# Expert rows added by TensorE with diagonal gates, all tiles gathered early, and a channel norm in two groups

## What is computed

```python
def conv_module(xn, ...):
    a, g = split(xn @ w_pw1 + b_pw1)
    u = a * sigmoid(g)
    dw = causal depthwise conv of width 31 over (state, u)
    z = silu(layer_norm(dw, ln_g, ln_b))     # over the 1024 channels
    return z @ w_pw2 + b_pw2

def hier_moe(xn, ...):   # 4 groups of 8 experts, 2 experts a row
    y[n] = sum over the row's two experts e of
           gate[n, e] * ((silu(xn @ w_gate[e]) * (xn @ w_up[e])) @ w_down[e])

x = x + mixer(rms_norm(x));  x = x + hier_moe(rms_norm(x))     # both layers
y = rms_norm(x)
```

## Time and profile before

| | us |
|---|---|
| median of three runs | 1279.34 |
| lowest and highest | 1275.59, 1279.53 |
| the profiled execution, its own time | 1276.34 |
| its span, first to last instruction | 1274.7 |
| TensorE busy in the span | 1076.6 |
| VectorE busy | 493.8 |
| ScalarE busy | 289.6 |
| Pool busy | 271.8 |

### The profile page before, as it was taken

One profiled execution on the slowest core, in us unless ns is written; L12 is line 12 of the kernel. 1 busy time (PEld: TensorE's weight loads), 2 busy tenths in 40 slices (PEclk: granted clock), 3 DMA queues, 4 the chain that ended last, 5 costly groups with the idle time before them and its releaser, 6 DMA issues.

```text
span 1274.7 us, 14566 instructions
## 1 busy us (share of the span) xinstructions
PE 1076.6 (84%) x5326; PEld 626.3 (49%) x5326; DVE 493.8 (39%) x1066; ACT 289.6 (23%) x616; POOL 271.8 (21%) x289
## 2 busy tenths in 40 slices
PE   6999999999996879888765999987987978787780
PEld 5777777774545333333325777743545333233320
DVE  3244444444356111111116699994555111111116
ACT  3233232233111101000003455554111101000002
POOL 3000000001002211111032388860003111011033
PEclk9999999999997999888886999998996989888995
DMA  8953322302706999999955922100027999999973
GB/s 273 387 182 110 109 93 77 103 30 106 298 34 225 398 419 420 420 421 421 418 188 137 363 66 66 34 24 1 34 84 280 411 420 420 421 419 421 397 269 131
DMA packets 107791, 303.67 MB, mean 238 GB/s; under 512 B 18248, under 2 KB 65480, under 8 KB 82745
## 3 DMA queue, kind: packets, MB, share of 16 engines
q1 hardware_dynamic: 85481, 254.74, 51.7%
q0 software_dynamic: 22256, 48.22, 10.5%
HBM read 278.34 MB, written 57.12 MB: 263 GB/s over the span
## 4 chain that ended last, share of the span: by engine, by line
PE 58%; DMA 21%; DVE 10%; issue 8%; ACT 2%; SPq 1%; POOL 0%; DVEq 0%; POOLq 0%
DMA ring<-in_w_up 16%; PE bank L1205 12%; PE bank L522 10%; PE bank L421 7%; PE bank L1222 7%; PE bank L549 4%; DVE bank L1688 2%; PE bank L1484 2%; PE bank L572 2%; PE bank L1195 2%; PE bank L588 2%; PE bank L613 2%; PE bank L346 1%; DMA work<-in_w_pw 1%; PE bank L954 1%
## 5 line engine op out<-in xcount | busy, mean ns | idle before, releaser
L1205 PE MATMUL bank<-ring,work 128*64 128x512 f32 x704 | 171.2, 642 | 30.9 <-DMA ring<-in_w_up 29.1
L1222 PE MATMUL bank<-ring,work 128*64 128x512 f32 x528 | 127.9, 629 | 37.1 <-DVE work L1241 21.6
L1484 PE MATMUL bank<-arena,work 128*128 128x288 f32 x512 | 129.4, 415 | 8.4 <-issue 4.0
L522 PE MATMUL bank<-arena,ring 128*128 128x288 f32 x512 | 131.9, 412 | 0.0
L1205 PEld LDWEIGHTS bank<-ring,work 128*64 128x64 f32 x704 | 60.6, 147 | 138.9 <-issue 136.6
L1237 DVE TENSOR_TENSOR work<-work,bank 128x256 f32<-128x256 f32 x33 | 13.9, 421 | 287.3 <-ACT work L1233 287.3
L1484 PEld LDWEIGHTS bank<-arena,work 128*128 128x128 f32 x512 | 99.1, 195 | 38.2 <-issue 8.4
L1635 POOL TENSOR_TENSOR ring<-ring 128x606 f32<-128x606 f32 x76 | 103.8, 1365 | 55.6 <-ACT ring L1584 46.0
L522 PEld LDWEIGHTS bank<-arena,ring 128*128 128x128 f32 x512 | 94.9, 190 | 32.6 <-issue 7.9
L421 PE MATMUL bank<-ring,arena 128*128 128x512 f32 x224 | 101.1, 605 | 6.6 <-ACT arena L1619 6.6
L1205 PE MATMUL bank<-arena,work 128*64 128x512 f32 x352 | 86.5, 648 | 17.1 <-DMA arena<-in_w_up 16.1
(11 more groups left out here) (258 smaller groups left out, 1299.6 us busy)
## 6 DMA issues: line engine op xcount, KB each, us to landing
ring<-in_w_down SPq DMA_DIRECT2D x32, 2048.0 KB, 24.2
ring<-in_w_gate SPq DMA_DIRECT2D x22, 2048.0 KB, 21.6
ring<-in_w_up SPq DMA_DIRECT2D x22, 2048.0 KB, 28.2
arena<-in_w_gate SPq DMA_DIRECT2D x10, 2048.0 KB, 23.9
arena<-in_w_up SPq DMA_DIRECT2D x10, 2048.0 KB, 31.6
ring<-in_w_qkv SPq DMA_DIRECT2D x24, 512.0 KB, 6.0
y_sorted<-gain POOLq DMA_DIRECT2D x8, 1536.0 KB, 5.7
work<-in_w_pw SPq DMA_DIRECT2D x16, 512.0 KB, 5.1
```

What stands on the lines that cost most here:

```text
L522: mm = nc.tensor.matmul(bank[b][:, 0:HT], wa[s][:, w, c, :], xt[:, c, h * HT:(h + 1) * HT], start=c == 0, stop=c == C - 1)
L1205: mm = nc.tensor.matmul(bank[2 + s][rr, :], xte[s][:, c, rr], wgu[g][:, :, e, c, :], start=c == 0, stop=c == C - 1)
L1222: mm = nc.tensor.matmul(bank[5 + h][rr, :], hts[:, c, rr], wdn[s][:, e, c, h * HALF:(h + 1) * HALF], start=c == 0, stop=c == FC - 1)
L1484: mm = nc.tensor.matmul(bank[banks[h][w]][:, 0:GT], wp[s][:, w, c, :], xt[:, c, h * GT:(h + 1) * GT], start=c == 0, stop=c == C - 1)
```

## The change

- **Adding the rows.** VectorE builds ten diagonal matrices from the gates (`spread_gates`) when the experts are done. TensorE multiplies them with the gathered rows into PSUM (`mix_pe`: four products of 128x512 a tile), and VectorE adds the sum to x in one pass. TensorE's order in the boundary: sum 0, sum 1, turn 0, sum 2, turn 1, sum 3, turn 2, sum 4, then the gated products; tiles 3 and 4 are turned inside their second half, the small vectors inside the first. VectorE's order: add 0, add 1, norm 0, add 2, norm 1 and so on. ScalarE now copies both halves of the turned tiles.
- **Gathers.** Tile 0's blocks lie in the free end of `arena`, so all ten blocks have a place and are fetched early (tile 4's behind the last store), and ten late gathers follow.
- **Convolution weights.** The buffers in `work` are regrouped so that the first chunk's weights fit once pair 14's first products are done; the second chunk's wait for the last add.
- **Channel norm.** The variance, root, reciprocal, scaling and Silu run over rows 0 to 255, then over rows 256 to 575.
- The warm-up products now start with `extra_end` in both layers, and the table for the root is loaded ahead.

```diff
+        y_at = [[arena[:, FIRST_Y + k * D:FIRST_Y + (k + 1) * D]] +
+                [ring[:, 1, (2 * j + k) * D:(2 * j + k + 1) * D] for j in range(TILES - 1)] for k in range(2)]
...
-        xe = part[0:2]
+        xe = part[0:4:2]
...
+        xte = [a.rearrange("p (c r) -> p c r", c=C) for a in part[1:4:2]]
+        gate_diag = work[:, 2 * D:2 * D + 2 * TILES * P].rearrange("p (k j n) -> p k j n", k=2, j=TILES)
...
         def norms_act(act, steps, n):
+            if n == 2:
+                nc.scalar.activation(warm[:], eps[:], ACT.Sqrt)
+                for j, turn in ((0, None), (1, 0), (2, 1), (3, 2), (4, 3), (None, 4)):
+                    if j is not None:
+                        norm_act(act, steps, n, j)
+                    if turn is not None:
+                        turn_act(act, n, turn)
+                        turn_copy(act, nc.scalar.copy, n, turn, 1, turn_ev_d)
+                return
...
         def norms_dve(dve, steps, n):
+            if n > 0:
+                for j in range(TILES + 1):
+                    if j < TILES:
+                        combine_dve(dve, n // 2 - 1, j)
+                    if j >= 1:
+                        norm_dve(dve, steps, n, j - 1)
+                return
...
-            do(V.tensor_copy(slot[:], slot_f[:]))
...
                 if local == EARLY_PAIRS:
                     pool.wait_ge(further_known, 2 * (l + 1))
+                    pool.wait_ge(far_scattered, 16 * (2 * TILES - FAR_FIRST) * (l + 1))
...
+                    for j in range(TILES - 1):
                         for k in range(2):
+                            y_rows_in(pool, j, k, early_slot)
+            for k in range(2):
+                y_rows_in(pool, TILES - 1, k, early_slot)
...
+                pool.wait_ge(gathered[j], 64 * l + 32)
                 for k in range(2):
+                    y_rows_in(pool, j, k, late_slot)
...
+        def mix_pe(pe, l, j):
             r = rows[j]
+            if j == 0:
+                pe.wait_ge(gates_spread, l + 1)
+            pe.wait_ge(gathered[j], 64 * (l + 1))
+            if j >= 2:
+                pe.wait_ge(combined, TILES * l + j - 1)
+            for h in range(2):
+                for k in range(2):
+                    mm = nc.tensor.matmul(mix_out(j)[:, h * HALF:(h + 1) * HALF], gate_diag[0:r, k, j, 0:r],
+                                          y_at[k][j][0:r, h * HALF:(h + 1) * HALF], start=k == 0, stop=k == 1)
+            mm.then_inc(mixed, 1)
...
+        def combine_dve(dve, l, j):
+            here = x[0:rows[j], j, :]
+            dve.wait_ge(mixed, TILES * l + j + 1)
+            nc.vector.tensor_tensor(here, here, mix_out(j), ALU.add).then_inc(combined, 1)
...
         def experts_pe(pe, l):
...
             extra_turns(pe, l, further)
+            pe.wait_ge(extra_end, l + 1)
+            keep_running(7, 16)
+            if l == LAYERS - 1:
+                for j in range(TILES):
+                    mix_pe(pe, l, j)
...
+            if l == 0:
+                sp.wait_ge(base.gu_mm, EPAIRS - 1)
+                conv_load(sp, 0, 0)
             sp.wait_ge(base.dn_mm, EPAIRS * (l + 1) - 1)
...
         def conv_first(sp):
-            sp.wait_ge(gathered[0], landed(0, 1))
-            conv_load(sp, 0, 0)
+            sp.wait_ge(gathered[0], 64)
...
+            sp.wait_ge(combined, TILES)
             conv_load(sp, 1, 1)
...
-            pe.wait_ge(combined, 1)
-            for j in range(HALF_TILES):
-                keep_running(4 if j else 10)
...
-                turn_pe(pe, 2, j)
+            mix_pe(pe, 0, 0)
+            for j in range(TILES - 1):
+                mix_pe(pe, 0, j + 1)
+                if j < HALF_TILES:
+                    turn_pe(pe, 2, j)
...
             for c in range(C):
                 pe.wait_ge(sq_done, c + 1)
+                mm = variance(c, 0)
+                if c < C - 3:
+                    variance(c, 1)
+            mm.then_inc(var_mm, 1)
+            for c in range(C - 3, C):
+                mm = variance(c, 1)
             mm.then_inc(var_mm, 1)
...
+            for g, (at, end) in enumerate(LN_PARTS):
+                act.wait_ge(var_mm, g + 1)
+                nc.scalar.activation(sig[:, at:end], bank[6 + g][:, 0:end - at], ACT.Sqrt, bias=ln_eps[:]).then_inc(std_done, 1)
+            for g, (at, end) in enumerate(LN_PARTS):
+                for c in range(C):
+                    act.wait_ge(scaled, C * g + c + 1)
+                    nc.scalar.activation(dw[:, c, at:end], dw[:, c, at:end], ACT.Silu, bias=chan[:, c, TAPS + 2:TAPS + 3],
+                                         scale=chan[:, c, TAPS + 1:TAPS + 2]).then_inc(swished, 1)
...
+            for g, (at, end) in enumerate(LN_PARTS):
+                dve.wait_ge(std_done, g + 1)
+                steps.done(V.reciprocal(sig[:, at:end], sig[:, at:end]))
+                for c in range(C):
+                    V.tensor_tensor(dw[:, c, at:end], dw[:, c, at:end], sig[:, at:end], ALU.mult).then_inc(scaled, 1)
```

More of the change, by code:

```diff
@@ L152, in encoder @@
         up_i = sb("up_i", [P, CAP], I32)
-        slot = sb("slot", [P, 2, TILES], I32)
         r_iota = sb("r_iota", [P, CAP])
@@ L1146, in experts_pool @@
                     pool.wait_ge(further_known, 2 * (l + 1))
+                    pool.wait_ge(far_scattered, 16 * (2 * TILES - FAR_FIRST) * (l + 1))
                     pool.wait_ge(base.y_out[0], 16 * (EPAIRS // 2) * (l + 1))
                     pool.wait_ge(base.y_out[1], 16 * (EPAIRS // 2) * (l + 1))
-                    for j in range(TILES):
+                    for j in range(TILES - 1):
                         for k in range(2):
-                            if early(j, k):
-                                y_rows_in(pool, j, k, early_slot)
-        def early(j, k):
-            return k == 0 or j < EARLY_TILES
-        def landed(j, layers, late=True):
-            each = [1 + (late and early(j, k)) if late else early(j, k) for k in range(2)]
-            before = [1 + early(j, k) for k in range(2)]
-            return 16 * (sum(before) * (layers - 1) + sum(each))
+                            y_rows_in(pool, j, k, early_slot)
+            for k in range(2):
+                y_rows_in(pool, TILES - 1, k, early_slot)
         def y_rows_in(pool, j, k, part):
@@ L1171, in gather_pool @@
             for j in range(TILES):
-                pool.wait_ge(gathered[j], landed(j, l + 1, late=False))
+                pool.wait_ge(gathered[j], 64 * l + 32)
                 for k in range(2):
-                    y_rows_in(pool, j, k, late_slot if early(j, k) else slot)
-        def combine_dve(dve, steps, l, j):
-            r = rows[j]
-            dve.wait_ge(gathered[j], landed(j, l + 1))
-            steps.done(nc.vector.scalar_tensor_tensor(x[0:r, j, :], y_at[0][j][0:r, :], gate_w[0:r, 0, j:j + 1],
-                                                      x[0:r, j, :], ALU.mult, ALU.add))
-            nc.vector.scalar_tensor_tensor(x[0:r, j, :], y_at[1][j][0:r, :], gate_w[0:r, 1, j:j + 1],
-                                           x[0:r, j, :], ALU.mult, ALU.add).then_inc(combined, 1)
@@ L1227, in ex_turn_copy @@
             eng.wait_ge(m.xt_mm, i + 1)
-            copy(xte[s][:, 4 * half:4 * half + 4, :], bank[half][:].rearrange("p (c r) -> p c r", c=4)).then_inc(done, 1)
+            copy(xte[s if m is base else 1][:, 4 * half:4 * half + 4, :], bank[half][:].rearrange("p (c r) -> p c r", c=4)).then_inc(done, 1)
         def ex_silu_act(act, m, i, s):
```

86 lines of the change are left out of this document (47 added, 39 removed).

## The result

| | before | after |
|---|---|---|
| median of the runs, us | 1279.43 (1275.59 to 1280.24, 4 runs) | 1291.39 (1290.88 to 1292.33, 4 runs) |
| the profiled execution, us | 1276.34 | 1291.39 |
| its span, us | 1274.7 | 1289.7 |
| TensorE, VectorE busy, us | 1076.6, 493.8 | 1114.2, 482.1 |

The ratio after to before is 1.0091 with a 95% interval of 1.0071 to 1.0111: slower by 12 us between the medians. The profiled execution of before lies 3 us under its median and that of after on its own, so the two traces differ by 15.0 us.

A forecast was written before the change was run, and what follows sets the result against it. Bound taken: waits in the boundary between layers, no engine or transfer full, with VectorE's convolution behind. +14.9 - 6.2 + 2.5 = +11.2 us on the profiled 1276.34 gives 1287.5; 1289 taken for the median, range 1278 to 1300.

The forecast's parts named there:

- boundary and convolution: Between the layers and the convolution behind: later fifth norm delays the second chunk's weights, so the stage loses 14.9 us.
- channel norm: Two groups start the projection 5.15 us earlier and regain half of 2.0 us of clock: gain 6.2 us.
- end: Last layer's five sums on TensorE: last norm 2.5 us late, bounds 1.5 and 5.
- The order of the sums: Boundary: nothing overlaps between TensorE and VectorE; a cycle takes 7.6 us against 4.5, TensorE idle some 3.0 us in each.
- The clock: Boundary: each return of TensorE from three idle gaps costs 2.2 us, 6.6 in all; first gated half does not pay again.
- Rival (a): Clock holds through the three gaps: boundary 8.3, norm 7.2, sum +3.6, about 1281 us; chance 0.12.
- (b): Weights do not bind, the queue's 10 MB go faster: boundary costs 9.9, sum +6.2, 1283 to 1285 us; chance 0.12.
- (d): Clock holds and weights do not bind together: -1.4 us, 1275 to 1278, or an unseen gain; chance 0.10.
- (c): Clock stays at 1.2 GHz through every sum after the gaps: 9 to 12 us more, 1298 to 1301; chance 0.10.
- Two more gathers and the early weights at nothing: Ahead of the late gathers: both cost nothing; other bound, load beside the gathers, 3 us on the last stored rows.
- the late gathers themselves later than before: Sign at the boundary's start that the forecast was wrong: then the early weights cost; no size given.
- The weights bind: Second chunk: 10 MB stream follows the fifth norm, 14.9 us late, and VectorE's wait grows by the difference.

The follow-up runs named there:

- Experiment 2: Changed kernel with each turn one sum later on TensorE (sum 2 ahead of turn 0 and so on): ratio 0.9994 to the kernel before, span 1276.9 us.
- Experiment 3: Changed kernel with nine unit-matrix products in each of TensorE's three waits for a tile's norm: ratio 1.0087 to the kernel before, span 1285.7 us.
- experiment 6: Changed kernel with the last layer's sums back on VectorE, without diagonals and warm-up there: ratio 1.0095 to the kernel before, span 1290.3 us.
- Experiment 10: Changed kernel with the first chunk's convolution weights issued once tile 0's rows are in: ratio 1.0059 to the kernel before, span 1282.5 us.
- experiment 4: Changed kernel with the convolution's small vectors sent after the last tile's gathers: ratio 1.0077 to the kernel before, span 1290.1 us.
- experiment 5: Changed kernel with tile 4's two early gathers issued just ahead of its late ones: ratio 1.0137 to the kernel before, span 1295.3 us.
- experiment 8: Changed kernel with sums back on VectorE in both layers and second chunk's weights not held back: ratio 0.9943 to the kernel before, span 1270.1 us.
- experiment 11: Changed kernel with sums on VectorE, second chunk's weights not held back, small vectors after the last tile's rows: ratio 0.9906 to the kernel before, median 1267.07 us.
- Experiment 1: Kernel before with only the channel norm in two groups: ratio 0.9957 to the kernel before, span 1271.7 us.
- experiment 12: As experiment 11, with the first chunk's weights issued once tile 0's rows are in: ratio 0.9896 to the kernel before, median 1266.65 us.

## Why the prediction was right, and where it was off

The forecast was slower, 1289 us in a range of 1278 to 1300; it is 1291.39. The parts stand against the traces so:

| step | foretold | measured |
|---|---|---|
| boundary and convolution | +14.9 | +20.0 |
| channel norm | -6.2 | -6.7 |
| end | +2.5 | +1.7 |
| sum | +11.2 | +15.0 |

**The order of the sums: right.** The cycle was to be 7.6 us with 3.0 us of idle TensorE; it is 7.3 with 2.71, released by VectorE's norm. The product against a diagonal was put at 0.865 us, 3.46 a tile. It is 3.60 for one tile alone and 3.5 within a block. The add out of PSUM, in no row before, takes 1.22, the lower bound. Experiment 2 takes the cycle away and gets 12 us back, so the mechanism is shown.

**The clock: right in kind, wrong in place and size.** The step was 2.2 us for each of three gaps, 6.6 in all. In the profiled execution the clock held through all three and fell once, behind them: 3.4 us in sum 4 before the first gated product, and 1.7 in that product, which the forecast had said would not pay again. Experiment 3 takes both away. The price of the same gaps was 1.7 to 5.1 us in five executions, so no price per gap fits, and why the clock falls at one of them and not at another stays open. Rival (a), that the clock holds, was right for three cycles and wrong for the last sum. Of (b) and (d) the weights speak: TensorE waited 6.81 us for them. (c) had the clock low through every sum after the gaps. No execution shows this; that of experiment 6 comes nearest, with sums 2 and 3 partly low.

**"Two more gathers and the early weights at nothing": wrong, and the largest error.** The forecast argued from a mean: DMA 0.17 busy at 644 to 648, so the load lies in a hole. It gave 3 us as the other bound and did not take it. The issue of its two transfers took the sync engine 7.4 us from 639.60 on (1.3 before), the late gathers came 1.9 us late, and the forecast's own sign ("the late gathers themselves later than before") was there to see. What it had not seen is the second step. The small vectors wait for tile 0's rows. In the kernel before the weights stand ahead of them on the queue, and they follow tile 1's first gather by 3.1 us. With the weights gone from there they follow it by 1.7, and sum 1 waits 2.48 us and runs slower by 1.8. The first turn ends at 688.95 where 682.5 was foretold: 6.4 us, 2.2 ahead of sum 0 and 4.2 in sum 1. Experiment 10 gives back 7.2 us of span, and experiment 4 gives back sum 1's share alone; experiment 5 says that the two gathers have hardly a part in it (6.85 us behind the store and not 7.1). The rule of the Trainium skill that the forecast cited (DMA: Bandwidth & Descriptors, Queues, rings and completion order: each DMA engine takes turns between the queues that have work) would, by the forecast's bound, have added 3 us, with which the sum would have been 1290.5. The runs here agree with it (the late gathers start 2.4 us later by the early load, 7.1 against 4.7 us behind the store), in sign and nearly in size, though no run shows that it is by taking turns. The choice against it was wrong, and the 3 us would still have left out sum 1's 4.2.

**How the two met.** At the first gated product 6.4 us too little for the start, 3.2 too much for the clock and 0.6 too much for two cycles leave 2.6: it was foretold for 707.8 and began at 710.44. So the 14.4 us there (11.8 foretold) are partly right by cancelling errors. The same holds for the clock: with the 1.8 in sum 1 it cost 6.9 us in all, close to the 6.6 booked, but in other places and in part for another wait.

**The weights bind: right, with 2.0 us missing.** The time from the fifth norm to the second chunk's product was taken as unchanged at 37.0 us. It is 39.0. Of this 1.2 is the second chunk's 1 MB, sent at 711.79 ahead of the router's tables: experiment 8 takes it away. The other 0.8 stays open. The first tap was foretold 9.9 us late (both halves of chunk 0 done at 726.3) and came 14.9 late; as VectorE then waits for the second chunk's weights anyway, this did not change the stage, and its wait grew by 5.2 us where 5.0 follow from the forecast. The fifth norm's terms add up to 712.1, where 712.2 is written. The sum of the boundary is 14.9 + 2.6 + 2.0, and 0.5 more arises up to the variances.

**The channel norm: right.** The projection starts 4.8 us earlier (5.15 foretold) and runs 2.0 us faster (1.0 foretold): all that the clock had cost there came back, not half. It does not in every execution: behind the same 2.6 us of idle time the projection took 22.3 to 22.4 us in experiments 4, 6 and 11, and 20.84 in the ten other traces. ScalarE's Silu begins at 888.18, where the table load of 1.28 us ends, and that load starts 0.01 us behind the second root's end. The 1.38 us of drain that the page ScalarE: Activation LUTs of the Trainium skill adds for a switch (What ACT_TABLE_LOAD costs) do not show in this row either; the row before was the better guide. Experiment 1 shows the gain by itself.

**The end: right, 0.8 us too dear.** The warm-up took 5.47 (5.3 foretold) and the five sums 17.5 (17.3). The last norm ends 26.2 us after the first late gather, before 24.5. Experiment 6 measures 1.8.

**The step to the median.** The sum was made against the profiled execution and 1.5 us were added for the median. The profiled execution of the kernel before lay 3 us low, and so the trace shows 15.0 us where the medians show 12.0.

## What to carry to other kernels

When work moves to another engine, write both engines' orders side by side and follow one item: if turn j needs norm j, which stands behind add j+1, which needs sum j+1, nothing overlaps, and moving the turn back by one sum can be worth more (12 us here) than the choice of the engine (4 to 6). A load put into a hole of the mean DMA busy share is not free if a short transfer that everybody waits for is issued in the 20 us behind it: price it by who waits for that landing, not by its bytes. Look too at what moves up in the queue when an issue is taken out of it, and send small transfers behind the last gather that is waited for. When a producer comes to end later, look at what now stands ahead of the next stream in the queue.

## What the runs showed of the hardware that was not expected

- The granted clock stayed full through three idle gaps of 2.71 us with 4.6 us of work between them. It fell near 703.6 (0.89 on the mean of 702 to 704), with TensorE back at work since 702.40, and stayed at 0.50 through a busy stretch. With 2.17 us of products in each gap it did not fall. In two other executions with the same gaps (experiments 4 and 6) it fell after the second gap (in sum 3), in experiment 6 after the first as well, and was full again in sum 4. The rows of one gap, or of one execution, would not have told this.
- Seven transfers of 66 rows in all (31, five single ones and 30 rows of 4 KB, 264 KB), sent 1.7 us behind tile 1's gathers, held tile 1's rows back by 2.5 us and more, though the DMA engines were on the mean 0.35 busy in that stretch. The rows landed 8.3 to 9.5 us after their first gather in the seven executions with these transfers there, within 4.1 in experiment 11 with nothing there, and after 5.7 with two transfers of 512 KB there (experiment 12):

```profile
672.00:680.00 8.00, 5.52 (x21) 3.25 (x21) 1.22 (x1) 1.44 (x3) 6.03 (x7) 0.93 0.35 91
```

- What waits for a store of 512 KB started 2.4 us later because 1 MB had been sent 20 us before it, with pair 15's expert weights and the early gathers under way between them (experiment 10). In four of the ten executions with this load TensorE also waited 3.1 us for pair 15's up weights, and no more than 1.5 in the ten others. Which of these queues up behind which was not tried.
